# A 128-byte tile ahead of the weight ring of a two-layer trunk

## The chip, the cores and the metric

The kernel runs on one core of one Trainium2 chip. The metric is the device time of one execution in microseconds (us). Its engines are TensorE (PE, with PEld for the loading of its stationary operand), VectorE (DVE), ScalarE (ACT), GpSimd (POOL) and SyncE (SP), and 16 DMA engines move data between the device's memory and the core's on-chip memory, which has 128 partitions. A tile is addressed by a byte offset that is the same in all its partitions.

## The reference

Two layers, 256 tokens of width 1024, all in float32. Every sub-layer has an RMS norm ahead of it and one behind it, then the residual is added.

```python
D_MODEL = 1024; SEQ = 256; DEPTH = 2
POOL_WINDOWS = (2, 4, 8, 16); N_HEADS = 16
D_FF_DENSE = 2816; N_EXPERTS = 8; TOP_K = 2; D_FF_EXPERT = 3584

def swiglu(h, w_gate, w_up, w_down):
    return (jax.nn.silu(h @ w_gate) * (h @ w_up)) @ w_down

def reference(x, norm_g, pool_w, pool_scale, attn_w_in, attn_b_f, attn_w_out,
              ffn_w_gate, ffn_w_up, ffn_w_down,
              moe_w_router, moe_w_gate, moe_w_up, moe_w_down):
    for i in range(DEPTH):
        slot = i // 2
        h = rms_norm(x, norm_g[i, 0])
        if i % N_MIXERS == 0:
            y = pool_mixer(h, pool_w[slot], pool_scale[slot])
        else:
            y = forgetting_attention(h, attn_w_in[slot], attn_b_f[slot], attn_w_out[slot])
        x = x + rms_norm(y, norm_g[i, 1])
        h = rms_norm(x, norm_g[i, 2])
        if i % 2 == 0:
            y = swiglu(h, ffn_w_gate[slot], ffn_w_up[slot], ffn_w_down[slot])
        else:
            y = moe_swiglu(h, moe_w_router[slot], moe_w_gate[slot], moe_w_up[slot], moe_w_down[slot])
        x = x + rms_norm(y, norm_g[i, 3])
    return x
```

`moe_swiglu` gives each token the two experts with the largest router logits, weighted by a softmax over the two. The weights of all eight experts are needed, 8 x 3 x 1024 x 3584 floats, 352 MB, and they are most of what the kernel reads.

## The kernel before

All weights come through one ring of places on chip. A place holds one unit, 128 partitions of 2048 floats (`UNIT`), 1 MiB; ten places are the tile `raw`, the first tile allocated, and four more are `raw_extra`, the last one (`EXTRA_SLOTS`), used for the experts alone. SyncE issues the loads, in the order in which TensorE uses the units, by `load` (L520) in the first three parts and by `load_e` (L581) for the experts; ahead of each load it waits until the unit that was in the place has been used. A row of a load is 2,048, 4,096 or 8,192 bytes in one partition, depending on the unit.

Where float32 accuracy is needed at a higher rate, a unit is split. ScalarE copies it to `w_hi` in a rounded form (`split_hi`, L640), VectorE subtracts this from the unit and writes the rest back to the unit's own place, named `raw_lo` (`split_lo`, L971), and TensorE multiplies three times (L1479 to L1481: high by high, low by high, high by low). `w_hi` has three places. In the dense layer and the attention, `w_hi_h`, `w_hi_q` and `w_hi_v`, which stand in memory that is free then, are three more.

The order of the work is pooling mixer, dense SwiGLU, attention, experts. The experts come in pairs, four of them here: the first of a pair has 128 token places and is computed with split weights, the second has 64 and is computed from the unsplit unit (`in_b`, L1861, and `down_b`, L1874). 42 units belong to each expert, 84 to a pair. Where one pair follows on another, the first unit of the next pair must have landed and been split before TensorE can begin with it. The loads of the next pair have been queued by then, as far as places were free.

Tiles are allocated one behind the other. The helper `sb` reserves a tile for the whole program; a tile opened by a `with` block is given back at its end, so that the next one begins at the same byte. Ahead of `raw_extra` there is already an unused tile of 64 bytes, `to_raw_extra`. These are the lines around the change and around the second block of the ring:

Of the kernel before, what the change touches and what calls it, by code (L numbers as in the profile page):

```python
# [8 lines left out]
P = 128  # L9
# [106 lines left out]
def trunk(nc, x_d, norm_g, pool_w, pool_scale, w_in, b_f, w_out, ffn_gate, ffn_up, ffn_down,  # L116
# [9 lines left out]
    with ExitStack() as ctx:  # L126
        def sb(name, shape, dt=f32):
            return ctx.enter_context(nc.sbuf_tensor(name, shape, dt))
# [2 lines left out]
            return ctx.enter_context(nc.semaphore(name))  # L131


        with nc.sbuf_tensor("raw_lo", [P, RAW_SLOTS, UNIT], f32r) as raw_lo:
            pass
        raw = sb("raw", [P, RAW_SLOTS, UNIT])
# [1998 lines left out]
```

## Time and profile before

| | us |
|---|---|
| three runs, median | 1243.45 |
| three runs, lowest and highest | 1242.34, 1243.51 |
| the profiled execution | 1243.32 |
| its span, first to last instruction | 1241.5 |
| TensorE busy in the span | 1205.1 |
| VectorE busy | 687.0 |
| ScalarE busy | 539.7 |
| data moved by DMA | 413.52 MB, mean 333 GB/s |

The span is cut into stages by the times in the trace: pooling and dense layer to about 210 us, attention to about 345, the router to about 375, the four pairs of experts to about 1230, and the last norm and the stores to the end. The page gives the share of busy time of each engine and of the DMA engines in 40 slices; a share near 1 of two resources at once says only that either may set the time, and the places where one waits for the other tell which.

### The profile page before, as it was taken

The numbers are of one execution on the slowest core, as the hardware profiler recorded it, in microseconds if no ns is written. First come the engines' busy times: TensorE is split into PE (matmuls) and PEld (weight loads), VectorE is DVE, ScalarE is ACT, GpSimd is POOL, SyncE is SP. The second block draws the span as 40 slices with busy tenths as digits, with TensorE's granted clock in tenths as the row PEclk, the third lists the DMA queues.
The fourth block names the chain that finished last, engine by engine and source line by source line (L and its number), as shares of the span: only waits on it lengthen the run. The fifth ranks groups of instructions, "written<-read, shape, count | busy, mean of one in ns | idle before, by whom it ended". The sixth has DMA issues, their size and how long they took to land.

```text
span 1241.5 us, 15258 instructions
## 1 busy us (share of the span) xinstructions
PE 1205.1 (97%) x5922; PEld 847.8 (68%) x5922; DVE 687.0 (55%) x761; ACT 539.7 (43%) x525; POOL 141.2 (11%) x141
## 2 busy tenths in 40 slices
PE   9999999989989999999999999899999989999996
PEld 8888887778878888335788833578883357887332
DVE  4944455746578987102888610378861038896102
ACT  3743335445546776002677500267750036775001
POOL 0000000000026260200006020000602000050200
PEclk9999999999979999999999999999999999999999
DMA  9965554754367999999999999999999999999994
GB/s 287 367 191 182 189 184 129 204 164 135 103 254 276 367 364 348 365 407 413 411 413 409 409 409 405 414 412 414 408 407 407 407 414 413 413 408 405 411 407 199
DMA packets 128279, 413.52 MB, mean 333 GB/s; under 512 B 10753, under 2 KB 30209, under 8 KB 113794
## 3 DMA queue, kind: packets, MB, share of 16 engines
q1 hardware_dynamic: 127394, 409.28, 86.4%
q0 software_dynamic: 816, 3.28, 0.8%
q8 instruction: 49, 0.80, 0.3%
q14 instruction: 20, 0.16, 0.0%
HBM read 411.48 MB, written 1.05 MB: 332 GB/s over the span
## 4 chain that ended last, share of the span: by engine, by line
PE 84%; DVE 7%; DMA 6%; SPq 1%; ACT 1%; issue 1%; DVEq 0%; ACTq 0%
PE bank L1479 19%; PE bank L1481 19%; PE bank L1480 19%; PE bank L1861 14%; DMA raw<-in_moe_w_gate 5%; PE bank L1874 4%; DVE raw_lo L971 3%; PE bank L1813 1%; PE bank L1941 1%; PE bank L1895 1%; SPq L581 1%; PE bank L1486 1%; DMA head_row<-in_heads 1%; PE bank L1737 1%; DVE y L1390 1%
## 5 line engine op out<-in xcount | busy, mean ns | idle before, releaser
L971 DVE TENSOR_TENSOR raw_lo<-raw,w_hi 128x2048 fp32r<-128x2048 f32 x148 | 338.0, 2304 | 76.3 <-ACT w_hi L640 75.8
L640 ACT ACTIVATE w_hi<-raw 128x2048 fp32r<-128x2048 f32 x149 | 284.5, 1916 | 129.6 <-PE bank L1481 79.0
L1479 PE MATMUL bank<-w_hi,h_hi 128*128 128x512 f32 x568 | 227.5, 400 | 13.6 <-DVE h_lo L1334 9.1
L1480 PE MATMUL bank<-raw_lo,h_hi 128*128 128x512 f32 x576 | 226.6, 393 | 0.0
L1481 PE MATMUL bank<-w_hi,h_lo 128*128 128x512 f32 x568 | 223.8, 394 | 0.0
L1861 PE MATMUL bank<-raw,h_b 128*64 128x512 f32 (+1 forms) x768 | 143.1, 523 | 0.0
L1479 PEld LDWEIGHTS bank<-w_hi,h_hi 128*128 128x128 f32 x568 | 107.9, 190 | 44.7 <-issue 15.3
L1480 PEld LDWEIGHTS bank<-raw_lo,h_hi 128*128 128x128 f32 x576 | 109.3, 190 | 22.4
L1481 PEld LDWEIGHTS bank<-w_hi,h_lo 128*128 128x128 f32 x568 | 107.8, 190 | 23.5
L971 DVE TENSOR_TENSOR raw_extra_lo<-raw_extra,w_hi 128x2048 fp32r<-128x2048 f32 x48 | 113.1, 2377 | 14.6 <-ACT w_hi L640 14.4
L1861 PEld LDWEIGHTS bank<-raw,h_b 128*64 128x64 f32 x768 | 53.6, 137 | 82.5 <-issue 73.9
L640 ACT ACTIVATE w_hi<-raw_extra 128x2048 fp32r<-128x2048 f32 x48 | 92.1, 1919 | 19.4 <-PE bank L1481 19.4
L927 ACT ACTIVATE silu<-bank 128x512 f32<-128x512 f32 (+1 forms) x16 | 8.7, 544 | 209.3 <-PE bank L1861 209.3
L1479 PE MATMUL bank<-w_hi,aT_hi 128*128 128x512 f32 x232 | 93.2, 402 | 0.1
L1481 PE MATMUL bank<-w_hi,aT_lo 128*128 128x512 f32 x232 | 91.7, 395 | 0.0
L1435 DVE COPY aT_b<-bank 128x512 f32<-128x512 f32 (+1 forms) x16 | 10.0, 625 | 141.4 <-PE bank L1949 141.4
L74 POOL TENSOR_TENSOR gpos_next<-gpos,slots_step 128x4 f32<-128x4 f32 x8 | 4.4, 549 | 653.7 <-PE bank L1884 653.7
L1874 PE MATMUL bank<-raw,aT_b 128*64 128x512 f32 x320 | 70.7, 592 | 0.0
L1431 DVE TENSOR_TENSOR act<-silu,bank 128x512 f32<-128x512 f32 (+1 forms) x16 | 9.9, 622 | 89.4 <-PE bank L1861 89.4
L1861 PE MATMUL bank<-raw_extra,h_b 128*64 128x512 f32 x256 | 57.4, 595 | 0.0
L1480 PE MATMUL bank<-raw_lo,aT_hi 128*128 128x512 f32 x144 | 56.8, 394 | 0.0
L1874 PEld LDWEIGHTS bank<-raw,aT_b 128*64 128x64 f32 x320 | 23.0, 137 | 44.0 <-issue 43.4
(320 smaller groups left out, 1621.5 us busy)
## 6 DMA issues: line engine op xcount, KB each, us to landing
raw<-in_moe_w_gate SPq DMA_DIRECT2D x96, 1024.0 KB, 14.4
raw<-in_moe_w_up SPq DMA_DIRECT2D x80, 1024.0 KB, 15.2
raw<-in_moe_w_down SPq DMA_DIRECT2D x64, 1024.0 KB, 14.9
raw_extra<-in_moe_w_down SPq DMA_DIRECT2D x48, 1024.0 KB, 16.4
raw_extra<-in_moe_w_up SPq DMA_DIRECT2D x32, 1024.0 KB, 13.2
raw_extra<-in_moe_w_gate SPq DMA_DIRECT2D x16, 1024.0 KB, 11.5
raw<-in_ffn_w_gate SPq DMA_DIRECT2D x11, 1024.0 KB, 5.5
raw<-in_ffn_w_up SPq DMA_DIRECT2D x11, 1024.0 KB, 5.3
```

Source lines behind the costliest of these rows:

```text
L581: sp.dma_start(blocks_of(raw_slot(s), n), src).then_inc(raw_in[s], 16)
L640: nc.scalar.activation(to, raw_slot(source), ACT.Copy).then_inc(hi_ready, 1)
L971: nc.vector.tensor_tensor(lo_slot(source), raw_slot(source), high.bitcast(f32), ALU.subtract).then_inc(lo_ready, 1)
L1390: nc.vector.tensor_tensor(y[:, tb, cols], y[:, tb, cols], bank[4 + 2 * tb + half][:, :], ALU.add).then_inc(acc_done, 1)
L1479: mm(out, a_hi, b_hi, start=first, stop=False)
L1480: mm(out, a_hi, b_lo, start=False, stop=False)
L1481: return mm(out, a_lo, b_hi, start=False, stop=last)
L1486: mm(to[:, 0:P], source, source, start=True, stop=True)
L1737: mm(logits(i, b), qk[h0:h0 + HD, b * P:(b + 1) * P], qk[h0:h0 + HD, T:T + (b + 1) * P], start=True, stop=False)
L1813: step = mm(bank[6 + k * slots // HALF][:, at:at + slots], xn[:, tb, k * P:(k + 1) * P], sel[:, tb, 0:slots], start=(tb == 0), stop=(tb == 1))
L1861: step = mm(to[t * CAP_B:(t + 1) * CAP_B, 0:n], h_b[:, k, :], w[:, i, t * n:(t + 1) * n], start=(k == 0), stop=(k == KB - 1))
L1874: step = mm(bank[4][t * CAP_B:(t + 1) * CAP_B, :], aT_bs[s % 2][:, m * P + g * CAP_B:m * P + (g + 1) * CAP_B], w[:, i, t * HALF:(t + 1) * ...
```

## The change

One unused tile is reserved ahead of the ring, 32 floats in each of 128 partitions, 128 bytes per partition.

```diff
--- before.py
+++ after.py
@@ -131,6 +131,7 @@
             return ctx.enter_context(nc.semaphore(name))
 
 
+        sb("to_raw", [P, 32])
         with nc.sbuf_tensor("raw_lo", [P, RAW_SLOTS, UNIT], f32r) as raw_lo:
             pass
         raw = sb("raw", [P, RAW_SLOTS, UNIT])
```

Every tile behind it begins 128 bytes later in each partition. As the program is built, `raw` moves from byte 16,512 to 16,640 and `raw_extra` from 196,224 to 196,352.

## Rows read from the trace of the kernel before

**Rows 1.** The page: span, DMA share and GB/s in 40 equal slices.

```profile
span 1241.5 us, 15258 instructions
...
DMA  9965554754367999999999999999999999999994
GB/s 287 367 191 182 189 184 129 204 164 135 103 254 276 367 364 348 365 407 413 411 413 409 409 409 405 414 412 414 408 407 407 407 414 413 413 408 405 411 407 199
```

**Rows 2.** Stretches (length, busy us (x instructions) by engine, clock, DMA share, GB/s).

```profile
375.00:586.00 211.00, 208.07 (x997) 134.99 (x995) 117.94 (x94) 92.50 (x69) 54.80 (x49) 1.00 0.96 366
586.00:802.00 216.00, 211.41 (x999) 136.39 (x1000) 117.27 (x77) 93.32 (x70) 25.38 (x26) 0.99 1.02 410
```

**Rows 3.** DMA queues, 586:802: packets; queue: packets, MB, share of 16 engines.

```profile
DMA packets 21416, 88.58 MB, mean 410 GB/s; under 512 B 1353, under 2 KB 1353, under 8 KB 17822
...
q1 hardware_dynamic: 21406, 88.43, 102.1%
```

**Rows 4.** The chain of waits, 575:590: start us, us, what.

```profile
559.96 21.47 DMA raw<-in_moe_w_gate
...
581.46 1.92 ACT w_hi L640
...
583.40 2.29 DVE raw_lo L971
```

**Rows 5.** Timeline of TensorE: start, us, line, operation [idle us before, releaser].

```profile
586.39 0.47 PE L1479 MATMUL bank<-w_hi,h_hi 128*128 128x512 f32 x1 [2.77 <-DVE h_lo L1334]
...
599.62 0.50 PE L1479 MATMUL bank<-w_hi,h_hi 128*128 128x512 f32 x1 [1.04 <-DVE raw_lo L971]
...
801.80 0.47 PE L1479 MATMUL bank<-w_hi,h_hi 128*128 128x512 f32 x1 [3.16 <-DVE h_lo L1334]
...
1017.24 0.50 PE L1479 MATMUL bank<-w_hi,h_hi 128*128 128x512 f32 x1 [3.19 <-DVE h_lo L1334]
```

**Rows 6.** A stretch where two pairs meet, columns as in rows 2.

```profile
583.00:600.00 17.00, 13.19 (x50) 8.77 (x47) 13.01 (x11) 10.64 (x9) 0.00 (x0) 0.90 1.03 409
```

**Rows 7.** DMA queues in 554:560 (2 KB rows), then 595:600 (4 KB rows).

```profile
DMA packets 1164, 2.32 MB, mean 387 GB/s; under 512 B 34, under 2 KB 34, under 8 KB 1163
...
q1 hardware_dynamic: 1163, 2.31, 104.9%
...
DMA packets 522, 2.03 MB, mean 406 GB/s; under 512 B 29, under 2 KB 29, under 8 KB 521
...
q1 hardware_dynamic: 521, 2.02, 101.1%
```

**Rows 8.** DMA queues in 4.2:4.8 (rows of x), then 6.3:6.56 (rows of bands).

```profile
DMA packets 69, 0.26 MB, mean 430 GB/s; under 512 B 6, under 2 KB 6, under 8 KB 69
...
q1 hardware_dynamic: 69, 0.26, 106.1%
...
DMA packets 16, 0.10 MB, mean 378 GB/s; under 512 B 0, under 2 KB 0, under 8 KB 16
...
q1 hardware_dynamic: 16, 0.10, 90.3%
```

**Rows 9.** Groups by line and form, 40:230: tiles, xcount | busy us, mean ns.

```profile
L1479 PE MATMUL bank<-w_hi,h_hi 128*128 128x512 f32 x116 | 46.3, 399 | 0.0
...
L971 DVE TENSOR_TENSOR raw_lo<-raw,w_hi 128x2048 fp32r<-128x2048 f32 x16 | 36.1, 2286 | 9.5 <-ACT w_hi L640 9.5
L640 ACT ACTIVATE w_hi<-raw 128x2048 fp32r<-128x2048 f32 x17 | 32.0, 1920 | 0.8 <-PE bank L1481 0.8
...
L1479 PE MATMUL bank<-w_hi_v,h_hi 128*128 128x512 f32 x44 | 17.3, 394 | 0.7 <-DVE aT_lo L1158 0.7
...
L971 DVE TENSOR_TENSOR raw_lo<-raw,w_hi_h 128x2048 fp32r<-128x2048 f32 x6 | 13.7, 2288 | 5.1 <-ACT w_hi_h L640 5.1
...
L640 ACT ACTIVATE w_hi_h<-raw 128x2048 fp32r<-128x2048 f32 x6 | 11.5, 1919 | 15.9 <-PE bank L1481 15.9
```

**Rows 10.** DMA queue in 1230:1241.5, the stores of out_x.

```profile
q1 hardware_dynamic: 576, 1.05, 24.4%
```

## The prediction

> **What bounds the kernel now.** I read the span and the DMA lines of the page first [rows 1]: 1241.5 us from the first to the last instruction, and from the 18th of the 40 slices to the last but one a DMA share of 9 and 405 to 414 GB/s. The profiled execution took 1243.32 us, so 1.8 us lie around the span; the median of the three runs shown is 1243.45, 0.13 above it, and I sum against 1243.32.
>
> The table of stretches [rows 2] shows the stage of the experts. In 586:802, one pair of experts, TensorE is busy for 211.4 of 216 us, and the DMA engines have a share of 1.02 at 410 GB/s (above 1, since packets on an engine overlap a little). Both resources are nearly full. Which one ends last can be seen where two pairs meet. The chain of waits [rows 4] goes there over a weight transfer: one MiB of `moe_w_gate` issued at 559.96 lands 21.5 us later, behind what is still queued. ScalarE splits it in 1.92 us and VectorE in 2.29 us, and only then can TensorE begin. The timeline of TensorE [rows 5] shows it idle for 2.77, 3.16 and 3.19 us at the three places where pairs meet, and each time 1.04 us once more some 13 us later (three such rows, one shown). Its clock also falls there, to a mean of 0.90 over 17 us [rows 6], because it had stood still: 1.7 us each. So the DMA engines end the pair, by 2.77 + 1.04 + 1.7 = 5.5 us or a little more, and within it TensorE fills the time. Over three places that is 12.2 us of idle time and 5.1 us of clock, 17.3 us in all: no faster weight stream can give more than this.
>
> That makes the kernel very sensitive to the time of one packet. In 586:802 the queue of the weights moved 21,406 packets [rows 3]; 1,353 are under 512 B and 20,053 carry data, 1,253 on each of 16 engines. One nanosecond less on each is 1.25 us a pair. The stream is already almost full in 375:586 (share 0.96 [rows 2]), so by the third meeting of pairs three such amounts have added up: 3.8 us per ns. About 0.2% (2.5 us) is the least that a measurement of this kernel tells from no change, and it stands for only 0.7 ns on packets of 164 ns.
>
> **The change, part by part.** It adds no instruction, removes none and moves none: built, the two programs have the same rows in the same order on all five engines, apart from line numbers that grow by one. No wait and no queue is touched. What is left is addresses. The ring `raw` began at byte 16,512 of a partition, that is 64 times 256 and 128 more; it now begins at 16,640, which is 65 times 256. Each place is 8,192 B, so all ten keep that offset, and the four of `raw_extra`, at 196,224 before, go to 196,352, again from 128 to 0 past a multiple of 256. Everything between moves by 128 too: `w_hi`, `x`, `h_hi`, `h_lo` go from 128 to 0, and `bands`, `scale`, `w_hi_q`, `w_hi_h`, `w_hi_v`, `silu_w`, `o_lo`, `v` go the other way, from 0 to 128. The trace of before therefore holds tiles at either offset, and they can be compared.
>
> *DMA writes into the ring.* A stretch in which only 2 KB rows arrive, 554:560, gives 104.9% of 6 us on 16 engines, 100.7 us for 1,129 data packets: 89.2 ns each [rows 7]. The stretch 595:600 with 4 KB rows gives 80.9 us for 492, 164.4 ns [rows 7] (the packets under 512 B are taken at nothing in all of these, so each value is slightly high). So 2,048 B more cost 75.2 ns, and about 14 ns of a packet don't grow with its size. An alignment could only take from those 14 ns. Now a tile at 0: `bands`, 768 KB on 128 partitions, has rows of 6,144 B, and 6.3:6.56 holds 16 packets of that size. They took 90.3% of 0.26 us on 16 engines, 234.8 ns each [rows 8]. In the same beginning `x`, at 128, arrives in 4 KB rows: 10.19 us for 63 packets, 161.7 ns [rows 8]. From `x`, a 6,144 B packet at 128 should take 161.7 + 75.2 = 236.9 ns; from the dense stretch 239.6. The tile at 0 is thus 2.1 ns below its neighbour in time, and 4.8 ns below the stretch with full queues. The first difference is nearly what the six small packets counted in with `x` would explain; most of the second is found in `x` as well, which stands at 128 and is 2.7 ns below the full stretch. I take **0 ns**, by the nearest pair (same beginning, same queue), and keep both ends: 4.8 ns less, and on the other side the 2.7 ns that full queues add to a packet at 128, which could grow with another placing. Sum for the writes: 0 us, ends -17.3 (capped) and +10.3 (2.7 x 3.8).
>
> A rule of the Trainium skill speaks for more. "DMA: Bandwidth & Descriptors", section "How a descriptor splits into AXI transactions", says that transactions must start at multiples of 256 B, so that a descriptor starting off one pays for the bytes from the boundary below. It is worded for reads. Were it to hold for writes, 128 B are 4 beats of 32 B; at the 850 MHz that the page gives for the fabric this is an estimate of 4.7 ns on every packet, and the stream would become faster than TensorE needs, for some 1226 us. The `bands` packets at 0 speak against it: by that rule they would lie 4.7 ns under the line through `x`, and they lie 2.1 at most.
>
> *DMA reads.* The only transfers that read from a moved tile into memory are the four stores of `out_x` at the end, from `x`. In 1230:1241.5 the queue held 24.4% of 11.5 us on 16 engines, 44.9 us, for 1.05 MB, which is 512 rows of 2 KB: at most 88 ns each [rows 10]. Even 4.8 ns less on each would be 32 x 4.8 ns = 0.15 us, spread over the four stores. I take 0.
>
> *Engines.* Stretch 40:230 has tiles of both kinds on the same lines [rows 9]. The subtraction L971 takes 2286 ns with `w_hi` (at 128) and 2288 with `w_hi_h` (at 0); the copy L640 takes 1920 ns into `w_hi` and 1919 into `w_hi_h`; the matmul L1479 takes 399 ns from `w_hi` and 394 from `w_hi_v`. Only the last pair differs, by 5 ns. If that were the alignment's, the 116 matmuls from `w_hi` in this stretch would gain 0.6 us and the others lose a part of it; in the experts' stage a few ns on a matmul are covered, since the DMA engines end the pair. I take 0, ends -0.6 and +0.6.
>
> **Sum:** 1243.32 + 0 = 1243.3 us.
>
> **The rivals.**
>
> *Faster: aligned writes are shorter.* A packet loses part of its 14 fixed ns. At the 4.8 ns bound the stream gains 3.8 x 4.8 = 18 us, more than the 17.3 that TensorE can follow, so the kernel ends at 1226; at the 2.1 ns bound it gains 8.0 us, 1235.3. For it: `bands` lies below every line, and nothing of a gain in the stream is lost until 17.3 us are used up. Against it: `x` at 128 lies below the full stretch as well. Chance 0.14, in equal parts.
>
> *Slower: more collisions in full queues.* All 14 places and the tiles that TensorE reads beside them now begin at 0 past 256. If the writes then meet the engines' reads more often, the 2.7 ns between the empty beginning and the full stretch grow. Place: 375 to 1014, where the stream never runs dry. Price 3.8 us per ns, with no cover at all, since the DMA engines already end each pair; from 0.7 ns per packet on it decides. Doubling the 2.7 ns gives 10.3 us, 1253.6. For it: this excess exists and nothing in the profile explains it. Against: the engines' own times show no such thing for tiles at either offset. Chance 0.11.
>
> *The change doesn't do what it says.* The addresses are those within a partition as the program has them; if the DMA hardware sees them with a base that isn't a multiple of 256, the places are no better aligned than before. It gives 1243.3 as well and is in the likeliest case.
>
> **How the numbers follow.** No effect: 0.75, at 1243.3, own range 1241.5 to 1245. Faster 0.14 (1226 to 1235), slower 0.11 (about 1247 to 1254). The range may leave out 0.2. To the likeliest case's 0.75 it needs the near parts of both others: I let it reach to a gain or a loss of about 1.5 ns a packet, 1.5 x 3.8 = 5.7 us, so 1238 to 1249, and count some 0.05 of the two rivals into it.
>
> **What would show it.** In the changed profile, stretches of the same kind as 554:560 and 595:600 should again give 89 and 164 ns a packet within 0.5, 586:802 should stay at 410 GB/s, and TensorE should be idle for about 3 us at each meeting of pairs. With the faster rival the packets of 4 KB fall to 160 to 162 ns, the stream shows over 415 GB/s or gaps, and the idle times shrink or vanish; with the slower one the idle times grow by over 1 us each. L971 on `w_hi_h` (now at 128) and on `w_hi` (now at 0) should keep 2288 and 2286. A time off by more than 0.2% with unchanged packets would mean that the argument missed a path on the engines' side.

## The result

The changed kernel takes 1234.99 us (median of four runs, 1234.32 to 1235.84), beside 1243.07 us for the kernel before (four runs). The ratio is 0.9931 with a 95% interval of 0.9909 to 0.9953: 8.1 us or 0.7% faster. The prediction was 1243.3 with a range from 1238 to 1249, so it missed, and on the side of its first rival. Measured twice more, on other chips, it gave 0.9933 [0.9913, 0.9953] and 0.9926 [0.9906, 0.9945].

The page of the changed kernel, its span, DMA share and GB/s in 40 slices, as in [rows 1]:

```profile
span 1233.8 us, 15258 instructions
...
DMA  9955553653376999899999999999999999999994
GB/s 296 361 184 192 180 195 116 198 185 109 109 279 244 370 364 366 334 420 421 422 422 421 419 393 419 423 422 423 419 408 392 420 422 423 422 419 387 397 421 189
```

Where the stream of the experts' weights is full it now moves 419 to 423 GB/s and no longer 405 to 414. New are slices of 387 to 408 between them. The stretches of [rows 2] and [rows 6], with the same columns:

```profile
375.00:586.00 211.00, 209.06 (x1003) 136.06 (x1003) 119.00 (x96) 93.89 (x71) 57.45 (x49) 1.00 0.96 368
583.00:600.00 17.00, 14.44 (x62) 9.95 (x59) 14.94 (x12) 10.02 (x7) 0.00 (x0) 1.00 1.03 421
586.00:802.00 216.00, 213.10 (x1015) 137.91 (x1014) 120.32 (x77) 95.28 (x69) 25.42 (x26) 1.00 1.02 417
```

The packets are shorter. These are the DMA queues in the changed kernel in 554:560 (2 KB rows) and 595:600 (4 KB rows), as in [rows 7]:

```profile
DMA packets 1226, 2.44 MB, mean 407 GB/s; under 512 B 38, under 2 KB 38, under 8 KB 1225
...
q1 hardware_dynamic: 1225, 2.43, 104.8%
...
DMA packets 545, 2.11 MB, mean 421 GB/s; under 512 B 32, under 2 KB 32, under 8 KB 544
...
q1 hardware_dynamic: 544, 2.10, 102.1%
```

By the same working as for before (share of the 16 engines' time over the packets of 512 B and more), 100.6 us over 1,187 data packets are 84.8 ns (89.2 before) and 81.7 us over 512 are 159.5 ns (164.4 before): 4.4 and 4.9 ns less. Now the beginning, 4.2:4.8 with the rows of `x` (now at 0) and 6.3:6.56 with those of `bands` (now at 128), as in [rows 8]:

```profile
DMA packets 70, 0.25 MB, mean 423 GB/s; under 512 B 8, under 2 KB 8, under 8 KB 70
...
q1 hardware_dynamic: 70, 0.25, 104.6%
...
DMA packets 18, 0.11 MB, mean 425 GB/s; under 512 B 0, under 2 KB 0, under 8 KB 18
...
q1 hardware_dynamic: 18, 0.11, 101.2%
```

`x` takes 10.0 us for 62 packets, 162.0 ns, and took 161.7 at 128. `bands` takes 4.21 us for 18, 233.9 ns, and took 234.8 at 0. In the beginning the alignment makes no difference for `x`: windows of 0.5 to 0.8 us around this one all give 161.5 to 162.7 ns in both kernels. The reading of `bands` is coarser. In the kernel before, 6.3:6.6 in place of 6.3:6.56 holds 19 packets at 240.8 ns. The 4 to 5 ns are there only later, where the stream runs in full.

The timeline of TensorE where pairs meet, as in [rows 5]:

```profile
585.02 0.47 PE L1480 MATMUL bank<-w_hi,h_hi 128*128 128x512 f32 x1 [1.53 <-DVE h_lo L1335]
...
596.70 0.50 PE L1480 MATMUL bank<-w_hi,h_hi 128*128 128x512 f32 x1 [1.04 <-DVE raw_lo L972]
...
797.38 0.47 PE L1480 MATMUL bank<-w_hi,h_hi 128*128 128x512 f32 x1 [1.86 <-DVE h_lo L1335]
...
1009.72 0.47 PE L1480 MATMUL bank<-w_hi,h_hi 128*128 128x512 f32 x1 [1.92 <-DVE h_lo L1335]
```

It waits for 1.53, 1.86 and 1.92 us (2.77, 3.16 and 3.19 before), the waits of 1.04 us remain, and in 583:600 its clock stays at 1.00 (0.90 before). So it does behind the second meeting (1.00 in 797:814, where before has 0.90); behind the third it still fell (0.90 in 1008:1025). Three waits shorter by 3.8 us together and two falls of the clock fewer, 1.7 us each, make 7.2 of the 7.7 us by which the spans differ. The times of the engines' operations in the dense layer didn't move (L1480 to L1482 are L1479 to L1481 of before):

```profile
L1480 PE MATMUL bank<-w_hi,h_hi 128*128 128x512 f32 x116 | 46.3, 399 | 0.0
...
L1480 PE MATMUL bank<-w_hi_v,h_hi 128*128 128x512 f32 x44 | 17.3, 394 | 0.7 <-DVE aT_lo L1159 0.7
```

### The profile page after: what moved, and what is told of

It reads as the page before. It is cut to its first block, busy times and chain, and to the rows that moved or that the text cites. A ratio compares the mean times of both kernels' runs of the same rounds, so it can differ in the third digit from the quotient of the medians.

```text
span 1233.8 us, 15258 instructions
## 1 busy us (share of the span) xinstructions
PE 1201.3 (97%) x5922; PEld 845.5 (69%) x5922; DVE 686.5 (56%) x761; ACT 539.6 (44%) x525; POOL 144.0 (12%) x141
## 4 chain that ended last, share of the span: by engine, by line
PE 85%; DVE 7%; DMA 6%; ACT 1%; SPq 1%; issue 1%; DVEq 0%; ACTq 0%
PE bank L1480 19%; PE bank L1482 19%; PE bank L1481 19%; PE bank L1862 14%; DMA raw<-in_moe_w_gate 5%; PE bank L1875 4%; DVE raw_lo L972 3%; PE bank L1814 1%; PE bank L1942 1%; PE bank L1896 1%; PE bank L1487 1%; SPq L582 1%; DMA head_row<-in_heads 1%; PE bank L1738 1%; DVE y L1391 1%
## 5 line engine op out<-in xcount | busy, mean ns | idle before, releaser
L1480 PE MATMUL bank<-w_hi,h_hi 128*128 128x512 f32 x568 | 226.4, 399 | 9.8 <-DVE h_lo L1335 5.3
L1481 PE MATMUL bank<-raw_lo,h_hi 128*128 128x512 f32 x576 | 225.0, 391 | 0.0
L1482 PE MATMUL bank<-w_hi,h_lo 128*128 128x512 f32 x568 | 222.6, 392 | 0.0
L1480 PEld LDWEIGHTS bank<-w_hi,h_hi 128*128 128x128 f32 x568 | 107.1, 189 | 40.7 <-issue 11.5
L1481 PEld LDWEIGHTS bank<-raw_lo,h_hi 128*128 128x128 f32 x576 | 108.7, 189 | 21.9
L1482 PEld LDWEIGHTS bank<-w_hi,h_lo 128*128 128x128 f32 x568 | 106.9, 188 | 23.2
L1480 PE MATMUL bank<-w_hi,aT_hi 128*128 128x512 f32 x232 | 93.2, 402 | 0.0
L1482 PE MATMUL bank<-w_hi,aT_lo 128*128 128x512 f32 x232 | 91.8, 395 | 0.0
L1481 PE MATMUL bank<-raw_lo,aT_hi 128*128 128x512 f32 x144 | 56.8, 394 | 0.0
```

What stands on the lines that cost most here:

```text
L1480: mm(out, a_hi, b_hi, start=first, stop=False)
L1481: mm(out, a_hi, b_lo, start=False, stop=False)
L1482: return mm(out, a_lo, b_hi, start=False, stop=last)
```

## The experiments

### The stream alone

`stream_dst4k` computes nothing. SyncE alone sends 1 MiB units from the experts' weights to ten places, 28 units at each offset of the ring, and the eight offsets follow one another (shortened):

```python
for n in range(28):
    i = n % 10
    if n >= 10:
        sp.wait_ge(landed[i], 16 * count[i])
    place = ring[:, to + i * 2048:to + (i + 1) * 2048]     # to = 0, 8, 16, ... 56 floats
    sp.dma_start(place.rearrange("p (b n) -> p b n", n=1024), src).then_inc(landed[i], 16)
```

> No trunk is computed: SyncE alone streams 1 MiB units of moe_w_gate in 4 KB rows into ten places, 28 units at each of eight offsets of the ring past a multiple of 256: 0, 32, 64, ... 224 B; out_x is a copy of x. No engine touches on-chip memory. Theory A: at 0 the full rate, 421 GB/s (160 ns a packet); at 128 the rate of the kernel before, 409 (164 ns). If the bytes from the boundary below are paid for, the packet grows with the offset, by 1.2 ns per 32 B to 8 ns at 224; if it is one transaction more whatever the offset, seven equal values. Theory B, and D (the excess is the stream's writes meeting the engines' reads of the same places): the same 421 GB/s at all eight offsets.

The DMA queues in the midst of three of the eight parts, at 0, 32 and 224 bytes past a multiple of 256:

```profile
DMA packets 6014, 23.16 MB, mean 421 GB/s; under 512 B 360, under 2 KB 360, under 8 KB 6014
...
q1 hardware_dynamic: 6014, 23.16, 102.5%
...
DMA packets 5852, 22.55 MB, mean 410 GB/s; under 512 B 348, under 2 KB 348, under 8 KB 5852
...
q1 hardware_dynamic: 5852, 22.55, 102.5%
...
DMA packets 5840, 22.53 MB, mean 410 GB/s; under 512 B 340, under 2 KB 340, under 8 KB 5840
...
q1 hardware_dynamic: 5840, 22.53, 102.6%
```

At 0 a data packet takes 902 us / 5,654 = 159.5 ns and the stream 421 GB/s. At each of the seven other offsets it takes 163.9 to 164.4 ns (902 / 5,504 at 32 B) and the stream 410 GB/s. It is nearly the same amount whether 32, 128 or 224 bytes are off, and it is there without an engine at work: 4.4 to 4.9 ns, where the two kernels' full stretches differ by 4.9. So not the number of bytes ahead of the place counts, but whether it is off at all. What a packet spends the time on no run shows. The page "DMA: Bandwidth & Descriptors" of the Trainium skill, section "How a descriptor splits into AXI transactions", has it for reads that the bytes from the boundary below are paid for; by that 224 would cost seven times 32, and these rows disagree.

Each part begins with an empty queue, and so shows the beginning and the full stream at one offset. These are two stretches of the part at 128, 307.3:309.3, some 4 us after its first packets, and 311.3:313.3, some 8 us after them:

```profile
DMA packets 222, 0.84 MB, mean 422 GB/s; under 512 B 16, under 2 KB 16, under 8 KB 222
...
q1 hardware_dynamic: 222, 0.84, 102.8%
...
DMA packets 213, 0.82 MB, mean 408 GB/s; under 512 B 14, under 2 KB 14, under 8 KB 213
...
q1 hardware_dynamic: 213, 0.82, 102.0%
```

In the first a data packet takes 159.7 ns, as at 0, and in the second 164.0. The parts at 32, 64 and 96 pass from the one to the other 7 to 9 us after their first packets too. The price is not there from the first packet on, which is why `x` didn't show it. What sets it in, a longer queue or something else, isn't shown.

`stream_dst2k` is the same with rows of 2 KB.

> No trunk is computed: the stream alone in rows of 2 KB, at the same eight offsets of the ring; out_x is a copy of x. Theory A with a fixed cost per packet: about 407 GB/s at 0 (84 ns) and 387 at the seven others (88 ns), the same 4 ns as for rows of 4 KB. If the cost grew with the number of 256 B pieces of a packet, it would be half, 2 ns, 397 GB/s.

At 0 and at 32 bytes:

```profile
DMA packets 11317, 22.48 MB, mean 409 GB/s; under 512 B 341, under 2 KB 341, under 8 KB 11317
...
q1 hardware_dynamic: 11317, 22.48, 105.1%
...
DMA packets 9734, 19.34 MB, mean 387 GB/s; under 512 B 292, under 2 KB 292, under 8 KB 9734
...
q1 hardware_dynamic: 9734, 19.34, 104.4%
```

84.3 ns (924.9 us / 10,976) against 88.5 (835.2 / 9,442; 88.5 to 89.1 at the seven offsets): 4.2 ns for 2 KB, 4.4 for 4 KB. Between these two sizes the cost is one per packet and doesn't grow with it, so it weighs more on the shorter rows. Here it sets in some 4 to 5 us after the first packets of a part.

`stream_src4k` moves the rows' beginning in the device's memory instead (to 0, 32, 64, 128, 192 bytes past a multiple of 256, with the ring aligned), then the ring's alone, and then both (shortened; `off` is 0 in `stream_dst4k`):

```python
    src = w_d[0, e, 0:256, off + part * 1024:off + part * 1024 + 1024]     # off = 0, 8, 16, 32, 48 floats
```

> No trunk is computed: the same stream of 4 KB rows into the aligned ring, but the rows in the device's memory begin 0, 32, 64, 128 and 192 B past a multiple of 256; then the ring at 128 with the source at 0, the ring at 128 with the source at 128, and both at 0 again; out_x is a copy of x. If the side that reads pays as the side that writes, all stretches but the first and the last run at 409 GB/s; if only the writing side pays, stretches 1 to 5 and 8 run at 421 GB/s and 6 and 7 at 409; if what counts is that source and target have the same offset, 7 is fast as well.

Source at 192 with the ring at 0; ring at 128 with the source at 0; ring and source both at 128:

```profile
q1 hardware_dynamic: 5462, 21.05, 102.5%
...
q1 hardware_dynamic: 5738, 22.13, 102.7%
...
q1 hardware_dynamic: 5641, 21.73, 102.7%
```

These are 421, 410 and 410 GB/s (MB over 50, 54 and 53 us), and the source at 32, 64 and 128 gives 421 as well. In these streams only the side that writes on-chip memory pays, and an equal offset on both sides doesn't help.

### The ring and the other tiles apart

Four kernels compute the whole trunk with other addresses. `ring_only` aligns the fourteen places and keeps the other large tiles' offset from a multiple of 256, with two small tiles taken from behind to fill the place (against the changed kernel; the two lines are left out further down):

```diff
 sb("to_raw", [P, 32])
 raw = sb("raw", [P, RAW_SLOTS, UNIT])
+lg = sb("lg", [P, TB, E])
+top = sb("top", [P, TB, 8])
```

> Only the fourteen places of the ring go to multiples of 256; the small tiles lg and top (64 B each) now stand right behind raw, so that w_hi, x, h_hi, h_lo keep 128 past a multiple of 256 and bands, w_hi_h, w_hi_v keep 0, as in the kernel before. Theory A (the packets that write into the ring are longer when it stands off a multiple of 256): all of the gain, 1235 us, 4 KB packets at 160 to 161 ns and 421 GB/s in the full stretches. Theory B (what counts is that the tiles which the engines read and write beside the stream, w_hi, x, h_hi, moved): no gain, 1243 us, 164 ns. Half of both: near 1239 us.

`others_only` is its counterpart (against the changed kernel too):

```diff
-sb("to_raw", [P, 32])
 raw = sb("raw", [P, RAW_SLOTS, UNIT])
+sb("behind_raw", [P, 32])
...
-sb("to_raw_extra", [P, 16])
+sb("to_raw_extra", [P, 48])
```

> The counterpart: raw and raw_extra stay at 128 past a multiple of 256, all tiles between them stand as in the changed kernel. Theory A: 1243 us, 4 KB packets at 163.7 ns. Theory B: 1235 us, 160 to 161 ns.

`extra_only` is the kernel before with `to_raw_extra` at 48 floats, `pad64` has 16 floats in `to_raw`:

> Only the four places of raw_extra go to multiples of 256 (the unused tile ahead of them grows from 64 to 192 bytes); raw and all else as before. 96 of the 336 MiB of the experts go through them. Theory A: a share of 96/336 of the shorter packets, 0.29 x 8.1 = 2.3 us less, so 1240.8 us, and packets of one size in two groups of time. Theory B: 1243 us. A third one, C (the whole ring must be aligned, since a single late packet holds up its engine's queue): 1243 us with some packets short.

> An unused tile of 64 bytes in place of 128: raw and raw_extra stand at 192 past a multiple of 256. The streams alone showed one and the same packet time at all seven offsets other than 0, so by one transaction more whatever the offset: 1243 us, 4 KB packets at 163 to 164 ns, as at 128. If the bytes from the boundary below were paid for, 192 would cost 6 steps of 32 B where 128 costs 4: 2.3 ns a packet more, 8 us, 1251.

| kernel | ring off by | h_hi off by | ratio to before, 95% interval | runs |
|---|---|---|---|---|
| changed, measured three times | 0 | 0 | 0.9931, 0.9933, 0.9926 | 4, 6, 6 |
| `ring_only`, measured three times | 0 | 128 | 0.9966 [0.9945, 0.9987], 0.9958 [0.9938, 0.9978], 0.9964 [0.9947, 0.9981] | 7, 12, 12 |
| `others_only` | 128 | 0 | 1.0021 [1.0001, 1.0041] | 10 |
| `extra_only` | 128, extra places 0 | 128 | 0.9974 [0.9960, 0.9988] | 8 |
| `pad64` | 192 | 192 | 1.0004 [0.9990, 1.0018] | 10 |

The 4 KB stretch 595:600 of `ring_only`, and then of `others_only`:

```profile
DMA packets 536, 2.08 MB, mean 416 GB/s; under 512 B 32, under 2 KB 32, under 8 KB 534
...
q1 hardware_dynamic: 534, 2.06, 100.8%
```

```profile
DMA packets 528, 2.04 MB, mean 407 GB/s; under 512 B 31, under 2 KB 31, under 8 KB 528
...
q1 hardware_dynamic: 528, 2.04, 102.0%
```

By the same working 80.6 us over 502 data packets are 160.6 ns, and 81.6 over 497 are 164.2. In the same 5 us all kernels with the ring at 0 give 159.5 to 160.6 ns and those with it at 128 or 192 give 164.2 to 164.9, so the stream follows the ring's address. `pad64` shows no gain: 192 is as bad as 128. `extra_only` gives 3.2 us where 2.3 were expected from its 96 of 336 units, and the interval holds both; some slow packets don't spoil the rest.

But the time doesn't follow the ring alone. `ring_only` has the fast stream and stood above the changed kernel three times, twice of them beside it on one chip, and the last time with intervals that don't touch.

> The changed kernel once more, so that it and ring_only stand beside the same runs of the kernel before on one chip. Theory A (only the ring's alignment counts, and the 5 us between the two in separate looks come from chance falls of TensorE's clock where pairs meet and from differences between chips): ratio to before within 0.3% of that of ring_only. Theory B2 (the alignment of the other tiles adds to it): after_again at 0.993, ring_only at 0.997 of before.

> The fourteen places on multiples of 256, all other large tiles as before, measured again beside the changed kernel. Theory A: the same ratio as after_again. Theory B2: 0.4% above it.

> The changed kernel beside the two below on one chip. Theory A: 0.993 of before, and ring_only_third within 0.2% of it.

> Only the ring aligned. Theory A: equal to after_third, and the 0.3% by which it was slower twice is chance. Theory B2 (the other tiles' addresses give a part): again 0.3% above.

The matmuls of the first expert of a pair show why. This is the group of L1481 with `h_hi` in 600:640, at a granted clock of 1.00, mean ns of one behind the busy time, in `after_third`, `ring_only_third` and `others_only`:

```profile
L1481 PE MATMUL bank<-raw_lo,h_hi 128*128 128x512 f32 x37 | 14.4, 390 | 0.0
```

```profile
L1481 PE MATMUL bank<-raw_lo,h_hi 128*128 128x512 f32 x41 | 16.1, 394 | 0.0
```

```profile
L1481 PE MATMUL bank<-raw_lo,h_hi 128*128 128x512 f32 x41 | 16.1, 393 | 0.0
```

390 ns, and 394 or 393 where the ring and `h_hi` stand 128 bytes apart past multiples of 256, whichever of them is aligned. Two last kernels part `h_hi` from `w_hi`. `x_on` leaves `w_hi` at 0 and moves all from `x` on by 128 (`lg` and `top` behind `w_hi`); `w_hi_off` moves `w_hi` alone.

> The ring and w_hi at multiples of 256 as in the changed kernel; x, h_hi, h_lo, aT_hi and what follows 128 bytes on (lg and top stand behind w_hi), raw_extra at a multiple of 256. In ring_only and others_only the matmuls L1480 to L1482 with h_hi took 394 to 398 ns, in the kernel before and the changed one 390 to 395. If that comes from the distance of h_hi from the ring, 394 here in 600:700 and 0.3% above the changed kernel, 1238 us; if from w_hi's distance from the ring, 390 and 1234 us. The stream keeps 421 GB/s in either case.

> The counterpart: only w_hi stands at 128 past a multiple of 256, the ring and h_hi at 0 (lg and top ahead of w_hi, topi and mboth behind it). If h_hi's distance from the ring counts, 390 ns and 1234 us; if w_hi's, 394 and 1238.

The same group in 600:640 of `x_on`, then of `w_hi_off`:

```profile
L1481 PE MATMUL bank<-raw_lo,h_hi 128*128 128x512 f32 x40 | 15.8, 395 | 0.0
```

```profile
L1481 PE MATMUL bank<-raw_lo,h_hi 128*128 128x512 f32 x34 | 13.2, 389 | 0.0
```

`x_on` took 1239.0 us, 0.9954 [0.9931, 0.9977], with 395 ns; `w_hi_off` 1231.8 us, 0.9908 [0.9892, 0.9925], with 389 ns. The two ran beside each other, and their intervals don't touch. So for this group and for the time it is the distance of `h_hi` and `h_lo` from the ring that counts, not that of `w_hi`. (`w_hi` off by itself shows in the two other lines, 397 ns for `w_hi,h_hi` and 392 for `w_hi,h_lo` beside 394 and 390 in `after_third`, and the time didn't grow with it.) `extra_only` holds both distances in one trace, since there `h_hi` and the ten places stand at 128 and the four extra ones at 0:

```profile
L1480 PE MATMUL bank<-raw_extra_lo,h_hi 128*128 128x512 f32 x8 | 3.2, 395 | 0.0
```

It has 390 ns with `raw_lo` in the same 600:640, and in `after_third` `raw_extra_lo` takes 389. The sizes fit: 28 units of gate and up in each first expert, 12 split matmuls each, make 1,344 in four pairs, at 4 ns 5.4 us; `ring_only_third` and `after_third`, side by side, took 1238.7 and 1234.1 us. How an address does this to TensorE these runs don't tell. The kernel before has both tiles at 128 and the changed one both at 0, so this effect is no part of the difference between the two.

### What is left when the stream is not the limit

`half_late` loads only half of each row of the last 28 units of every second expert:

```diff
-                sp.dma_start(blocks_of(raw_slot(s), n), src).then_inc(raw_in[s], 16)
+                to = blocks_of(raw_slot(s), n)
+                if j % (2 * ROUND_UNITS) >= ROUND_UNITS + RAW_SLOTS + EXTRA_SLOTS:
+                    to, src = to[:, :, 0:n // 2], src[:, :, 0:n // 2]
+                sp.dma_start(to, src).then_inc(raw_in[s], 16)
```

> The changed kernel, but of the last 28 of the 42 units of each second expert only half the columns of each row are loaded (the place keeps older weights in the other half, so that the experts' outputs aren't the reference's): 14 of 84 MiB a pair less, all of it in the part where TensorE uses units faster than they arrive. It tells how much of the time the stream still sets. Theory A with the cap of the prediction (17.3 us below 1243.3): 1226 us, TensorE no longer idle where pairs meet. If the changed kernel is already limited by something else (the split of the first unit, which takes 1.9 + 2.3 us behind its landing, or the engines within the pair), it stays near 1234 us.

It took 1228.0 us, 0.9880 [0.9859, 0.9900]: 15 us less than before and by the ratios 6 to 7 less than the changed kernel. Its waits of TensorE in 375:1230 (who waited for whom: us in total, times, longest), and under them those of the changed kernel:

```profile
PE bank L1483 <- DVE raw_lo L975: 3.5, 4, 1.0
```

```profile
PE bank L1480 <- DVE h_lo L1335: 5.3, 3, 1.9
PE bank L1480 <- DVE raw_lo L972: 3.5, 4, 1.0
```

The waits for the first unit are gone, those of 1.0 us aren't: they were never the stream's. So the ceiling of the prediction, 17.3 us, was too high by 3 x 1.04 us, and what the stream can give at most is near 15 us.

Of these 15 us the alignment gave 8. Where the rest goes is seen where TensorE passes from the first expert of a pair to the second, at about 711. GB/s is the last column, the DMA share the one before; first the changed kernel, then the kernel before:

```profile
710.00:720.00 10.00, 10.00 (x44) 4.08 (x43) 0.69 (x1) 1.20 (x2) 0.00 (x0) 1.00 1.00 377
720.00:730.00 10.00, 10.00 (x43) 3.31 (x43) 3.01 (x5) 0.00 (x0) 0.00 (x0) 1.00 1.00 402
730.00:740.00 10.00, 10.00 (x48) 3.57 (x50) 1.12 (x2) 0.98 (x2) 6.26 (x13) 1.00 1.00 402
```

```profile
710.00:720.00 10.00, 10.00 (x45) 5.36 (x46) 0.69 (x1) 0.60 (x1) 0.00 (x0) 1.00 1.02 403
720.00:730.00 10.00, 10.00 (x40) 3.50 (x38) 2.75 (x4) 0.60 (x1) 0.00 (x0) 1.00 1.03 417
730.00:740.00 10.00, 10.00 (x47) 3.12 (x44) 0.69 (x1) 0.39 (x1) 6.24 (x13) 1.00 1.00 403
```

The kernel before keeps 403 to 417 GB/s here. In the changed one the stream falls to 377, 402 and 402, some 2 us short of the 421 that it has elsewhere (44, 19 and 19 GB/s less for 10 us each, over 421), and so in each pair (the slices of 387 to 408 on the page). Every load waits until the unit in its place has been used, so what fits these rows is that the faster stream has filled the fourteen places by the end of the first expert and must wait for the second one's first units to be used. `ring_only`, with the same stream and a slower TensorE, has the same stop and a larger one: 277 GB/s at a DMA share of 0.77 in 710:720. I changed no number of places to prove it. Of the 6.1 us a pair that 4.9 ns on 1,253 packets are worth, the distance from one meeting of pairs to the next kept 3.1:

```profile
794.39 2.29 DVE raw_lo L972
...
1006.72 2.29 DVE raw_lo L972
```

794.39 to 1006.72 is 212.3 us. Before, the same piece of the chain stands at 583.40 [rows 4] and, 215.4 us later, at 798.81. Those 3.1 us are a wait shorter by 1.3 and a fall of the clock less, 1.7. The stop accounts for 2 of the missing 3 us; the last 1 us I can't place.

### A version that is faster than both

In the changed kernel the first matmul of a pair waits for `h_lo`, behind `raw_lo`. `h_half_first` splits the first half of the gathered tokens ahead of the first unit:

```diff
-                    hi_e(ROUND_UNITS)
-                    he_hi(p, 1)
+                    he_hi(p, 1, [0])
+                    hi_e(ROUND_UNITS)
+                    he_hi(p, 1, [1])
...
-                    lo_e(ROUND_UNITS)
-                    he_lo(p, 1)
+                    he_lo(p, 1, [0])
+                    lo_e(ROUND_UNITS)
+                    he_lo(p, 1, [1])
```

> The changed kernel with another order where pairs meet: ScalarE and VectorE split the first half of the gathered tokens (h_hi, h_lo) before the first unit of the next pair, and the second half behind it. In the changed kernel the first matmul waits for h_lo, 0.7 us after raw_lo. If the landing still comes after the gather, it begins 0.3 to 0.6 us earlier at three places and the half-clock stretches become rarer: 1232 to 1234 us. If the landing comes before the gather (it came within 0.3 us of its end in the changed kernel), the copy of h_hi delays the split by 0.5 us and nothing is won: 1235 us.

> The changed kernel with the first half of the gathered tokens split before the next pair's first unit, beside the changed kernel on one chip: 0.9911 of before was measured, against 0.9931 to 0.9933 of the changed kernel in other calls. If the gain is real, 0.2% or some 3 us below after_third; otherwise equal to it.

It took 1231.3 us, 0.9911 [0.9895, 0.9927], and the second time 1230.0, 0.9903 [0.9882, 0.9924], beside 1234.1 of the changed kernel, 0.9926 [0.9906, 0.9945]: 4 us less, but the intervals overlap. `lo_before_acc` also lets VectorE form the fourth unit's low part before it adds the sums to `y`:

```diff
                     lo_e(ROUND_UNITS + 2)
+                    lo_e(ROUND_UNITS + 3)
                     ve.wait_ge(acc_done, p * 8 + 6)
                     accumulate(p * 8 + 4)
-                with pair_follows(ve, p, pairs):
-                    lo_e(ROUND_UNITS + 3)
```

> As h_half_first, and VectorE forms the low part of the fourth unit of the next pair before it adds the four results to y (2.5 us), not behind. Where pairs meet TensorE waits 1.04 us for that low part at three places: 3 us less than h_half_first if nothing else is late, so about 1228 us; if the stream or the sums into y are late next, no difference.

It took 1226.65 us, 0.9871 [0.9852, 0.9891]. Its waits of TensorE in 375:1230:

```profile
PE bank L1481 <- DVE raw_lo L973: 4.0, 4, 1.4
```

One wait is left at each meeting (1.1 to 1.4 us, the fourth is one of 0.4 us at the beginning of the experts), the one 12 to 13 us later is gone. The kernel is 16.7 us or 1.3% faster than the kernel before and 7.5 us faster than the changed one beside it, with intervals that don't touch.

## Why the prediction was wrong

**What bounds the kernel: right.** The DMA engines ended each pair, packets that are 4 to 5 ns shorter moved the whole kernel, and the waits named for it shrank.

**DMA writes into the ring: the step that failed.** The text set the value at 0 ns, "by the nearest pair (same beginning, same queue)". The comparison of `bands` at 0 with `x` at 128 was made in the first microseconds, and there nothing depends on the alignment: `x` takes 161.7 ns at 128 and 162.0 at 0. The right comparison was with full queues, and the number for it stood in the text: 239.6 - 234.8 = 4.8 ns, kept as an end of this term, left out of the range, and measured as 4.9. That it came so close is luck in part: with a window ending at 6.6 the same `bands` packets give 240.8 ns, and no difference. I explained most of it away, since `x` at 128 lay 2.7 ns below the full stretch too. That showed only that the cost is not there in the beginning. It was no reason to call it anything else in the full stream, the only place where it counted. Its opposite end, the 2.7 ns "which could grow with another placing", was this same cost with the wrong sign.

**The rule of the Trainium skill** ("DMA: Bandwidth & Descriptors", section "How a descriptor splits into AXI transactions") was weighed by the same comparison and refused for it. It gave an estimate of 4.7 ns for 128 bytes, close to what was measured. In its form it doesn't hold in these streams: the cost is on writes, a source off the multiple costs nothing, and 32 to 224 bytes cost the same. A price from a page that comes out at the unexplained part of a row deserved more than its half of the 0.14.

**The rate of 3.8 us per ns** is right as a sensitivity of the stream and too high for the time: 4.9 ns would be 18.6 us, capped at 17.3 or 1226 us, and 1235 was measured. It took a gain in the stream as kept until TensorE never waits. But the ring has only fourteen places, and the stream ran short where the second expert begins. The term to add was the room in the ring; about a third of the stream's gain seems to have gone there. The faster rival at its lower price of 2.1 ns came out at 1235.3, but only since one size was too small and the other too large.

**DMA reads and engines: right for this pair of kernels.** L1479 stayed at 399 and 394 ns, although the tiles changed sides. That "the engines' own times show no such thing for tiles at either offset" is right only as long as tiles move together: moved against the ring, `h_hi` costs 4 ns a matmul. The rows of before couldn't show it; their 5 ns between `w_hi` and `w_hi_v` are something else, since they stay when both change sides.

**The clock** was said to fall "because it had stood still". The length of the wait counts, but doesn't decide it. In the profiles of the four kernels with the ring wholly or in part off the multiple (waits of 2.8 to 3.2 us) it fell behind 10 of 12 meetings, and in the eight profiles of the changed kernel and `ring_only` (three each), `x_on` and `w_hi_off` (0.8 to 2.7 us) behind 4 of 24. In `others_only` TensorE waits for 3.20 and 3.14 us at the first two meetings, and its clock stays at 1.00 in 583:600 and 797:814. So the clock's 5.1 us in the ceiling, and its part of the gain, differ from one execution to the next.

**The range** counted 0.05 of the rivals and ended at 1238. With the unexplained 4.8 ns as an even chance it would have reached 1226.

## What to carry to other kernels

Where a long stream of DMA writes into on-chip memory sets the time, begin every row at a multiple of 256 bytes: here it is worth 4 to 5 ns a packet, about 2.7% at 4 KB and 5% at 2 KB, and costs one unused tile. Judge a suspected cost on rows in the state in which it would matter, here the stream in full, and let an excess that nothing explains stand as a possible gain. A faster stream seems to help only as far as the ring has room while its consumer is slow. The next gain lay in the order of the work where the consumer waits, 7.5 us beside 8.1.

## What the runs showed of the hardware

- A packet of 2 or 4 KB written off a multiple of 256 bytes takes 4.2 to 4.9 ns more once the stream has run for some 4 us (2 KB) or 8 us (4 KB), at any of seven offsets, and nothing more before that. The offset of the source, 32 to 192 bytes, costs nothing.
- The distance between the ring and `h_hi` past multiples of 256 changes the matmuls that read both from 389 or 390 to 393 to 395 ns, at the same clock. Its cause is open.
- TensorE's clock fell to the lower level, 1.2 GHz (a granted clock of 0.50 in 588:590 of the kernel before), behind some meetings of pairs and not behind others: it fell behind a wait of 1.92 us in the changed kernel, and it didn't behind 3.20 us in `others_only`. One such fall costs about 1.7 us [rows 6]. Single runs of one kernel lay up to 13 us apart (`ring_only`, second time, 1233.8 to 1247.1), and this may be a part of it.
